# A two-layer hybrid model on one core: projections with high and low parts, and as plain float32 products

## What is computed

```python
for layer in range(2):
    a = rms_norm(h, norm_mix[layer])
    if layer == 0:
        # a @ w_in (1024 x 3600): q, k, v with a short convolution -> gated delta rule (GDN)
        #                         z_b, xbc, dt                     -> state space part (SSD)
        h = h + hybrid_mixer(a, ...)          # ends with a product by 1024 x 1024
    else:
        # a @ w_in (1024 x 1840): queries, keys, values, gates -> three kinds of attention
        h = h + nsa_mixer(a, ...)             # ends with a product by 1024 x 1024
    a = rms_norm(h, norm_ffn[layer])
    u = causal_dwconv(a @ w_up, conv_w, conv_b)   # w_up is 1024 x 5632
    gate, up = split(u, 2)
    h = h + (silu(gate) * up) @ w_down            # w_down is 2816 x 1024
return rms_norm(h, norm_final)
```

## Time and profile before

| | before |
|---|---|
| median of 3 runs | 3439.76 us |
| the profiled execution, first to last instruction | 3455.9 us |
| PE busy | 3161.6 us, 91% |
| POOL busy | 1248.5 us, 36% |
| DVE busy | 1405.7 us, 41% |
| ACT busy | 938.8 us, 27% |
| mean granted clock of PE | 0.942 |
| moved by DMA | 127.46 MB |

### The profile page before, as it was taken

One profiled execution on the slowest core, in us unless ns is written; L12 is line 12 of the kernel. 1 busy time (PEld: TensorE's weight loads), 2 busy tenths in 40 slices (PEclk: granted clock), 3 DMA queues, 4 the chain that ended last, 5 costly groups with the idle time before them and its releaser, 6 DMA issues. The chain is left out here.

```text
span 3455.9 us, 41720 instructions
## 1 busy us (share of the span) xinstructions
PE 3161.6 (91%) x16629; PEld 2612.9 (76%) x16629; DVE 1405.7 (41%) x2167; ACT 938.8 (27%) x1447; POOL 1248.5 (36%) x638
## 2 busy tenths in 40 slices
PE   5967889887899999999897899999999899999998
PEld 4747887765778888888685787778878688888887
DVE  3675445353333133133301676655552332232334
ACT  3332223222133011021100454446661231010121
POOL 4325323465454444444642100000004544444442
PEclk8988999998899999999998897879999899999999
DMA  3100001110111111111114000000001111111111
GB/s 132 43 25 1 1 1 31 43 55 25 43 37 48 49 49 46 52 49 44 38 49 122 9 1 1 1 1 1 1 1 37 37 48 46 47 47 50 49 46 70
DMA packets 211543, 127.46 MB, mean 37 GB/s; under 512 B 8904, under 2 KB 208077, under 8 KB 211149
## 3 DMA queue, kind: packets, MB, share of 16 engines
q1 hardware_dynamic: 209600, 125.25, 12.3%
q10 hardware_dynamic: 1805, 0.28, 0.0%
HBM read 112.94 MB, written 8.39 MB: 35 GB/s over the span
## 5 line engine op out<-in xcount | busy, mean ns | idle before, releaser
L403 POOL TENSOR_TENSOR WH<-WR,ONES 128x1024 fp32r<-128x1024 f32 (+1 forms) x194 | 459.8, 2370 | 1355.1 <-PE PS L1312 1280.6
L1312 PE MATMUL PS<-YH,WH 128*128 128x512 f32 x2336 | 738.5, 398 | 63.5 <-POOL YL L428 34.9
L1312 PE MATMUL PS<-YL,WH 128*128 128x512 f32 x2336 | 726.6, 393 | 0.0
L1312 PE MATMUL PS<-YH,WL 128*128 128x512 f32 x2336 | 725.0, 392 | 0.0
L1312 PEld LDWEIGHTS PS<-YH,WH 128*128 128x128 f32 x2336 | 440.8, 190 | 178.5 <-issue 53.9
L1312 PEld LDWEIGHTS PS<-YL,WH 128*128 128x128 f32 x2336 | 444.0, 190 | 93.9
L1312 PEld LDWEIGHTS PS<-YH,WL 128*128 128x128 f32 x2336 | 442.5, 189 | 93.4
L406 POOL TENSOR_TENSOR WL<-WR,WH 128x1024 fp32r<-128x1024 f32 (+1 forms) x194 | 481.1, 2480 | 15.2
L1100 DVE SCALAR_TENSOR_TENSOR X<-PS,PTF,X 128x1023 f32<-128x1023 f32 (+1 forms) x176 | 225.6, 1282 | 573.4 <-ACT X L752 560.7
L752 ACT ACTIVATE X<-PS,PTF 128x1024 f32<-128x1024 f32 x88 | 106.2, 1207 | 840.5 <-PE PS L1312 840.3
L1670 PE MATMUL PS<-X,Z 128*128 128x64 f32 x2112 | 287.4, 287 | 0.0
(11 more groups left out here) (302 smaller groups left out, 3264.2 us busy)
## 6 DMA issues: line engine op xcount, KB each, us to landing
WR<-in_ffn_w_up_dram SPq DMA_DIRECT2D x88, 512.0 KB, 3.8
WR<-in_hy_w_in_dram SPq DMA_DIRECT2D x28, 512.0 KB, 3.8
WR<-in_ffn_w_down_dram SPq DMA_DIRECT2D x32, 448.0 KB, 3.6
WR<-in_ffn_w_down_dram SPq DMA_DIRECT2D x16, 512.0 KB, 3.7
WR<-in_nsa_w_in_dram SPq DMA_DIRECT2D x14, 512.0 KB, 3.7
Z<-in_x_dram SPq DMA_DIRECT2D x8, 512.0 KB, 7.5
xt_scratch<-H SPq DMA_DIRECT2D x1, 4096.0 KB, 12.1
H<-xt_scratch SPq DMA_DIRECT2D x1, 4096.0 KB, 12.3
```

The source lines that it names most:

```text
L403: pool.tensor_tensor(WH[:, slot, 0:k, :], WR[:, slot, 0:k, :], ONES[:, :].unsqueeze(1).broadcast_to([P, k, P]), ALU.mult).then_inc(w_hi, 1)
L1312: ins = pe.matmul(PS[:, 2 * slot + a, :], w[:, slot, i, :], y[:, i, a * HALF:(a + 1) * HALF], start=(i == 0 and w is WH and y is hi), stop ...
```

## The change

All projections become plain float32 products: one matmul per k-tile and 512 columns, with the weights as loaded and the inputs as computed. `WH`, `WL`, `YH`, `YL`, `MH`, `ML`, `GWH`, `GWL` and everything that fills them are gone, on POOL, ACT and DVE. The first half of an output tile is made over all k-tiles, then the second. Further:

- `WR` has 6 slots of 8 k-tiles (`RING`), and SP waits for the unit that last used a slot, by `gemm_done`; the load number of each unit comes from `first_load`.
- The inputs `Y` lie in `Z[:, 0:8]`, and DVE writes them from the norm directly. `U_HOUT` reads the mixed tiles in `X`. The transposed attention output is copied by ACT (even tiles) and DVE (odd tiles) in turn.
- All 22 hidden tiles have room (16 in `X`, 6 in `Z`), so the first projection runs as 44 units without a break and the second as 8 units of 22 k-tiles. There are 162 units. The loops over groups are written out.
- The scratch of the GDN and SSD parts moves to `Z[:, 8:16]`; the copy of `H` to DRAM and back is gone.

The diff, cut to its core:

```diff
-    GROUPS = [(0, 8), (8, 7), (15, 7)]
+    RING = 6
...
-    U_FFN = [36, 126]
-    U_NSA, U_NOUT = 104, 118
+    U_FFN = [36, 110]
+    U_NSA, U_NOUT = 88, 102
+    UNITS = 162
+    U_DOWN = [n + 2 * FT for n in U_FFN]
...
+        Y, SC = Z[:, 0:MT, :], Z[:, MT:2 * MT, :]
+        HT = SC.rearrange("p m (a n) -> p (m a) n", a=2)
+        WR = sb("WR", [P, RING, MT, P])
...
+        def hidden(k):
+            return X[:, k, :] if k < 16 else Z[:, MT + k - 16, :]
...
-            def load(n, slot, src):
+            def load(n, src):
 
-                if not isinstance(n, int) or n >= 2:
-                    sp.wait_ge(w_split, n - 1)
-                sp.dma_start(WR[:, slot, 0:src.shape[1], :], src).then_inc(w_loaded[slot], 16)
+                for b in range(-(-src.shape[1] // MT)):
+                    at = first_load[n] + b
+                    if at >= RING:
+                        sp.wait_ge(gemm_done, unit_of_load[at - RING] + 1)
+                    part = src[:, b * MT:min((b + 1) * MT, src.shape[1]), :]
+                    sp.dma_start(WR[:, at % RING, 0:part.shape[1], :], part).then_inc(w_loaded[at % RING], 16)
...
-            sp.dma_start(xt_scratch, HF).then_inc(spilled, 16)
...
-            def split(n, slot, k, loads):
-                pool.wait_ge(w_loaded[slot], loads)
...
-                pool.tensor_tensor(WH[:, slot, 0:k, :], WR[:, slot, 0:k, :], ONES[:, :].unsqueeze(1).broadcast_to([P, k, P]),
-                                   ALU.mult).then_inc(w_hi, 1)
-                pool.wait_ge(w_hi, n + 1)
-                pool.tensor_tensor(WL[:, slot, 0:k, :], WR[:, slot, 0:k, :], WH[:, slot, 0:k, :].bitcast(f32),
-                                   ALU.subtract).then_inc(w_split, 1)
...
-            for k in range(MT):
-                if k >= 4:
-                    act.wait_ge(gn_done, k - 3)
-                act.activation(YH[:, k, :], X[:, out_tile(k), :], ACT.Copy).then_inc(os_hi, 1)
...
-            for m in range(MT):
+            for m in range(0, MT, 2):
                 act.wait_ge(ot_ready, m + 1)
-                act.activation(YH[:, m, :], gemm_ps(m % 2), ACT.Copy).then_inc(ot_hi, 1)
+                act.activation(Y[:, m, :], gemm_ps(0), ACT.Copy).then_inc(ot_hi, 1)
...
-            def norm_apply(r, wcol, y0):
+            def norm_apply(r, wcol):
                 norm_factor(r)
                 for m in range(MT):
-                    if m >= 2:
-                        dve.wait_ge(y_ready, y0 + m - 1)
-                    dve.scalar_tensor_tensor(out=X[:, 17 + m % 2, :], in0=H[:, m, :], scalar=PTF[:, wcol + m:wcol + m + 1],
-                                             in1=PSF[:, 4 * HALF:6 * HALF], op0=ALU.mult, op1=ALU.mult).then_inc(yf_ready, 1)
+                    dve.scalar_tensor_tensor(out=Y[:, m, :], in0=H[:, m, :], scalar=PTF[:, wcol + m:wcol + m + 1],
+                                             in1=PSF[:, 4 * HALF:6 * HALF], op0=ALU.mult, op1=ALU.mult).then_inc(y_ready, 1)
...
+            def unit(n, moving, ready=None):
+
+                if n >= 2:
                     pe.wait_ge(psum_free, n - 1)
...
+                for a in range(2):
+                    for i in range(k_tiles(n)):
+                        at = first_load[n] + i // MT
+                        if a == 0 and i % MT == 0:
+                            pe.wait_ge(w_loaded[at % RING], 16 * (at // RING + 1))
+                        if a == 0 and ready is not None:
+                            ready(i)
+                        ins = pe.matmul(PS[:, 2 * (n % 2) + a, :], WR[:, at % RING, i % MT, :], moving(i)[:, a * HALF:(a + 1) * HALF],
+                                        start=(i == 0), stop=(i == k_tiles(n) - 1))
                 ins.then_inc(gemm_done, 1)
...
-                        for w, y in ((GWH, YH), (GWH, YL), (GWL, YH)):
-                            ins = pe.matmul(PS[0:count, 6 + a, :], w[:, i, 0:count], y[:, i, a * HALF:(a + 1) * HALF],
-                                            start=(i == 0 and w is GWH and y is YH), stop=(i == MT - 1 and w is GWL))
+                        ins = pe.matmul(PS[0:count, 6 + a, :], GWR[:, i, 0:count], Y[:, i, a * HALF:(a + 1) * HALF],
+                                        start=(i == 0), stop=(i == MT - 1))
```

More of the change, by code:

```diff
@@ L321, in ffn_loads @@
                 down = ffn_w_down[l].rearrange("(k p) n -> p k n", p=P)
[L322 to L338 removed]
+                for j in range(FT):
+                    load(U_FFN[l] + 2 * j, up[:, :, j * P:(j + 1) * P])
+                    load(U_FFN[l] + 2 * j + 1, up[:, :, (FT + j) * P:(FT + j + 1) * P])
+                columns(U_DOWN[l], down, 0, MT)
+            columns(U_QKV, w_in, 0, 12)
             columns(U_ZA, w_in, 1536, 4)
@@ L765, in _ @@
+            ffn(0, 1, U_HOUT)
+            norm(2, U_DOWN[0])
             act.wait_ge(slopes_ready, 1 + H16)
@@ L1070, in final_gain, with residual @@
                 dve.tensor_scalar(H[:, m, :], H[:, m, :], PTF[:, C_FIN + m:C_FIN + m + 1], None, ALU.mult).then_inc(fin_ready, 1)
-            def residual(n0, r, last):
+            def residual(n0, r):
                 for m in range(MT):
@@ L1076, in residual @@
                     dve.tensor_tensor(H[:, m, :], H[:, m, :], gemm_ps(n % 2), ALU.add).then_inc(psum_free, 1)
-                    if last and m >= 1:
+                    if m >= 1:
                         norm_sums(r, m - 1)
@@ L1474, in _ @@
                     pe.wait_ge(o_sb, TT)
-                unit(n, n % 2, MT, YH, YL)
+                unit(n, y)
                 pe.wait_ge(on_sq, h + 1)
```

303 lines of the change are left out of this document (89 added, 214 removed).

## The result

| | before | after |
|---|---|---|
| median of the paired runs | 3440.41 us (4 runs) | 3875.61 us (4 runs, 3867.81 to 3891.34) |
| profiled execution, span | 3455.9 us | 3889.6 us |
| PE busy, records | 3161.6 us | 3676.9 us, 13,557 |
| POOL busy | 1248.5 us | 206.7 us |
| moved by DMA | 127.46 MB | 119.23 MB |

The ratio is 1.127, with a 95% interval of 1.124 to 1.130: slower, by 435 us. The forecast was 3901 us, in a range of 3872 to 3950. PE records are matmul records of the profile; the last row is all DMA traffic of the execution.

A forecast was written before the change was run, and what follows sets the result against it. PE, busy 3161.6 of 3455.9 us, was taken to bound the kernel. A steady +564.0 us, less 103 us given back at the joints, made +461.4 us; 3439.8 + 461.4 = 3901 us, range 3872 to 3950.

The forecast's parts named there:

- the steady cost: All projections: every piece goes from 0.680 to 0.864 us, with the gate products +564.0 us in all.
- the joints: Places where PE waits: they give back 103 us; rival that they give nothing back, 4004 us, chance 0.06.
- a record is not two present matmuls: Rival, every projection record: a plain record costs two present ones, 0.4536 us instead of 0.432, 4034 us; chance 0.05.
- the second record does not stream at 0.2268: Rival, every unit: a product's second record streams at 0.2268 us, faster, held to about 2,700 us; chance 0.01.
- the clock held 1.00: Rival on PE's clock: plain products don't hold it, 0.86 us of stride per record, some 6,550 us; chance 0.01.
- a record takes 0.432 us: Sums of squares, line 1359: 12 records in gaps price a plain record at 0.432 us, a piece at 0.864 us.
- Norm to first unit: Four norms: DVE's first tile to the first unit's end falls from 23.6 to 18.1 us, -5.5 us each.
- Sums ahead of a norm: DVE's last two additions, 5.62 us beside POOL, take 1.23 each without it: -3.1 us three times, -2.1 in the first norm.
- The z gate and the output projection: Four z gate units +6.7 us; first output projection, its first unit -6.1 and seven units +20.5, together +14.4 us.
- After attention: Transposes with copies on ACT and DVE in parallel take 10.5 us, not 15.0: -4.5; eight units +23.5; together +19.0 us.
- The price of halves in turn: Norm to first unit: in turn 17.7 us, alternating 16.8 with cold start; elsewhere the order of halves is worth nothing.
- Delta rule, SSD, attention at 0: GDN, SSD and attention parts, outside the projections: untouched by the change, 0 us.

The follow-up runs named there:

- the order alone: Kernel before with only the loop order changed, first halves of all k-tiles ahead of second halves, three products kept: 3512.61 us, ratio 1.0202.
- the second median: The changed kernel timed once more without any edit, beside the experiments: 3868.21 us, ratio 1.1235 to the kernel before.
- the sign of one experiment: Changed kernel with its two loops exchanged so the halves of each k-tile alternate: 3884.64 us against 3868.21, but 6.6 us shorter outside attention.
- 4.4 and then 2 in another: Changed kernel with three slots for weight tiles instead of six: 3957.46 us, a single execution.

## Why the prediction was right, and where its size was off

**Slower, by the steady cost: right.** Two records a piece instead of three matmuls, PE never bound by anything else inside a run, POOL's disappearance worth nothing there. The rivals fell one by one: the joints did give time back; a record is not two present matmuls (0.4536 us), since the present ones pay nothing for a change of weights (the order alone left 663 in 150 us); the second record does not stream at 0.2268; and the clock held 1.00. Two of the prediction's arguments were weaker than they looked. That plain products hold the clock was argued from 20 us inside attention, but elsewhere in that stage of the same profile it is lower with PE just as busy (columns as in attention above):

```profile
2131.00:2231.00 100.00, 98.30 (x654) 0.81 0.00 1
```

The windows of the projections settle it, not that row. And that the two records of a piece are one per part of its weights, no view shows; they show two records and two weight loads.

**Inside the range, with some luck.** The forecast of 3901 us is 25 us above the first median, which lies inside the range by 3.6 us, and the second median lies 3.8 us below it. What separates the two is attention's clock, of which the prediction says nothing. The 16 us between span and median that it carried over are for the larger part the same thing, as far as two profiles tell: its profile had attention's longest value, 650.6 us, and the second one 10.3 us less.

**The size of a record: off, and the largest miss.** The step that failed is "a record takes 0.432 us", from 12 records in three short gaps of the earlier trace rows, with a unit's 10.89 us taken off. It takes 0.4288, outside the 0.430 to 0.434 that the prediction itself gave for being right. Why the short gaps read high is not shown. Over 6144 records the 0.0032 us are 19.7 us, more than the 12 that its bounds allowed for 0.002. Outside attention the first pair of profiles differs by 439.9 us, the forecast by 461.4; the record explains 19.7 of these 21.5. In the table it shows where it should: 6.8 us in each feed-forward part (2112 records, 6.2 missed), 1.5 in layer 1's inputs (1.5 missed). The Trainium skill's pages "TensorE: Matmul & The Clock Gate" (section "Back-to-back issue gap") and "FP8 and Floating Point Precision" (section "TensorE Precision Notes"), against which the prediction kept the rows, gave an estimate of +656 us for the steady part; by the measured record it is 3040 x (0.8576 - 0.6804) = +539 us. The estimate for a plain piece by these pages, 4 x 215.8 = 863 ns, is within 1% of the 858 ns found. What the estimate missed is the price of the present three matmuls, 680 ns against 3 x 215.8 = 647.

**The joints: right, to some 2 us a stage.** "Norm to first unit" had 18.1 us, it is 17.7. "Sums ahead of a norm" had 2.46 us for two additions, it is 2.50, and that POOL is the cause is shown. The z gate and the output projection, +18.0 with their norm, came to +18.0, though inside it the first unit ends later than I said: two products and 6.9 us of the second half were in the sum, and PE's restart after 3.96 us of waiting was not (12.1 us from the reciprocal's end to the unit's end, 10.4 in the sum); the cheaper record made up 1.2 us of it over the stage's 12 units. "After attention" had +15.9 with its norm and got +13.7.

**The price of halves in turn: the larger part missed.** I gave it 1.3 us at four norms and said that elsewhere the order of the halves is worth nothing. At three norms it is 0.7 to 0.9 us, and the larger part, 6.0 us, sits at the output projection. There tiles come late as well; the sum had the second half's 6.9 us in it, so the forecast has the term, but the statement was wrong.

**Delta rule, SSD, attention at 0.** SSD is (+0.2). The delta rule gave 2.7 us in the first pair of profiles and nothing in the second, about what two profiles of the kernel before differ by there (2.5 us). Attention's 0 was right for the kernel and wrong as a statement about two executions: its clock makes 5 to 29 us between them, and no bound of the range was meant for it.

**DMA.** Six loads ahead were ample, as said; four are enough too, three are not.

## What to carry to other kernels

Price a matmul by a long gapless window of the very form, and where there is only a short one, let the range carry its reading error times the count: here 3 ns times 6144 were the largest miss. Before two kernels are compared, cut both profiles at the same source lines: a stage that nobody touched moved by up to 29 us and would have turned the sign of one experiment. And price a wait of PE of some 4 us at 6 to 7, because the matmuls behind it run at the lower clock (3.92 us and then 2.6 in one experiment, 4.4 and then 2 in another).

## What was not expected

- Attention took 621.5, 636.7, 645.5 or 650.6 us (and 638.1 and 640.3) in thirteen profiles, several times the same value to 0.1 us in different programs, with granted clocks between 0.76 and 0.97 over 100 us while PE was busy for 89 to 98 of them. The runs scatter with it: 26 executions of the kernel before lay between 3426.8 and 3457.5 us. What chooses stays open.
- DVE beside POOL: operations with two SBUF tiles took 2038 to 2414 ns in the mean instead of 1220 to 1226, those with an operand in PSUM took the same beside POOL and without it (1220 and 1221 ns for the addition to `H`, 1280 and 1275 for a norm's tile).
- A float32r matmul of 512 columns takes 226.8 ns in every order tried. The record of a plain float32 one takes 428.8 ns, which is less than two of the former (453.6).
